# An attention output projection with Strassen's seven products for half of its rows of weights

## What is computed

```python
def mla(h, cos, sin, w_dq, q_norm_g, w_uq, w_dkv, kv_norm_g, w_ukv, w_o):
    ...
        outs.append(jnp.einsum('bhqk,bkhd->bqhd', p, v[:, :kend]))
    o = jnp.concatenate(outs, axis=1).reshape(B, S, H * V_HEAD_DIM)
    return o @ w_o

for i in range(DEPTH):                      # DEPTH = 2
    y = rmsnorm(h, attn_norm_g[i])
    y = conv_module(y, ...) if i == 0 else mla(y, ...)
    h = h + y
    h = h + swiglu(rmsnorm(h, ffn_norm_g[i]), ffn_w_gate[i], ffn_w_up[i], ffn_w_down[i])
return rmsnorm(h, final_norm_g)
```

## Time and profile before

| | us |
|---|---|
| median of 3 runs | 1991.01 |
| lowest, highest | 1988.06, 1994.06 |
| the profiled execution | 1993.24 |
| its span, first to last instruction | 1991.40 |

### The profile page before, as it was taken

One profiled execution on the slowest core, in us unless ns is written; L12 is line 12 of the kernel. 1 busy time (PEld: TensorE's weight loads), 2 busy tenths in 40 slices (PEclk: granted clock), 3 DMA queues, 4 the chain that ended last, 5 costly groups with the idle time before them and its releaser, 6 DMA issues.

```text
span 1991.4 us, 25065 instructions
## 1 busy us (share of the span) xinstructions
PE 1955.9 (98%) x9934; PEld 1671.0 (84%) x9934; DVE 1614.3 (81%) x1769; ACT 1141.2 (57%) x1138; POOL 227.7 (11%) x196
## 2 busy tenths in 40 slices
PE   8999899999999999999999999999999999999998
PEld 7999888888888888888888998888888888888886
DVE  6999886888888888888876775588888888888885
ACT  5898744555556555555544654355555555555553
POOL 0555400010011000110010000000010000101002
PEclk9999999999999999999999999999999999999999
DMA  8999464899998999889845444559989999999983
GB/s 272 257 259 236 148 214 148 240 271 278 254 235 241 261 279 262 223 242 263 258 145 151 123 143 174 190 174 287 243 216 273 259 279 239 236 253 262 277 211 127
DMA packets 253830, 453.37 MB, mean 228 GB/s; under 512 B 18708, under 2 KB 60444, under 8 KB 251420
## 3 DMA queue, kind: packets, MB, share of 16 engines
q1 hardware_dynamic: 207968, 349.73, 50.5%
q0 software_dynamic: 44256, 98.57, 28.8%
q10 hardware_dynamic: 1500, 3.61, 0.5%
HBM read 435.10 MB, written 2.10 MB: 220 GB/s over the span
## 4 chain that ended last, share of the span: by engine, by line
PE 87%; DMA 7%; DVE 3%; ACT 1%; issue 1%; SPq 0%; POOL 0%; ACTq 0%; DVEq 0%; POOLq 0%
PE ps L1802 83%; DMA raw<-in_conv_w_pw_dram 4%; DMA w_lo<-raw 3%; DVE ps L1311 1%; PE ps L2043 1%; ACT w_lo L772 1%; PE ps L2297 0%; PE ps L2298 0%; PE ps L2278 0%; DMA resid<-in_x_dram 0%; DVE w_lo L1188 0%; PE ps L1833 0%; SPq L557 0%; PE ps L1852 0%; PE ps L1841 0%
## 5 line engine op out<-in xcount | busy, mean ns | idle before, releaser
L1193 DVE TENSOR_TENSOR w_lo<-raw,w_hi 128x2048 fp32r<-128x2048 f32 x224 | 509.2, 2290 | 148.3 <-ACT w_hi L927 148.0
L927 ACT ACTIVATE w_hi<-raw 128x2048 fp32r<-128x2048 f32 x224 | 426.3, 1916 | 347.7 <-PE ps L1802 209.1
L1802 PE MATMUL ps<-w_hi,x_hi 128*128 128x512 f32 x1168 | 456.0, 390 | 0.9 <-DVE x_lo L1220 0.9
L1802 PE MATMUL ps<-w_hi,x_lo 128*128 128x512 f32 x1168 | 454.9, 389 | 0.0
L1802 PE MATMUL ps<-w_lo,x_hi 128*128 128x512 f32 x1168 | 454.8, 389 | 0.0
L1802 PE MATMUL ps<-w_hi,a_hi 128*128 128x512 f32 (+1 forms) x768 | 292.7, 381 | 0.0
L1802 PE MATMUL ps<-w_hi,a_lo 128*128 128x512 f32 (+1 forms) x768 | 292.3, 381 | 0.0
L1802 PE MATMUL ps<-w_lo,a_hi 128*128 128x512 f32 (+1 forms) x768 | 292.2, 380 | 0.0
L1802 PEld LDWEIGHTS ps<-w_hi,x_hi 128*128 128x128 f32 x1168 | 219.3, 188 | 47.1 <-DVE x_lo L1220 1.4
L1802 PEld LDWEIGHTS ps<-w_hi,x_lo 128*128 128x128 f32 x1168 | 219.3, 188 | 45.7
L1802 PEld LDWEIGHTS ps<-w_lo,x_hi 128*128 128x128 f32 x1168 | 219.3, 188 | 45.2
(11 more groups left out here) (242 smaller groups left out, 2992.7 us busy)
## 6 DMA issues: line engine op xcount, KB each, us to landing
raw<-in_ffn_w_down_dram SPq DMA_DIRECT2D x66, 1024.0 KB, 8.3
raw<-in_ffn_w_up_dram POOLq DMA_DIRECT2D x60, 1024.0 KB, 8.8
raw<-in_ffn_w_gate_dram SPq DMA_DIRECT2D x50, 1024.0 KB, 6.6
raw<-in_ffn_w_up_dram SPq DMA_DIRECT2D x48, 1024.0 KB, 6.4
row_bc<-in_ffn_w_gate_dram SPq DMA_DIRECT2D x38, 1024.0 KB, 5.9
raw<-in_conv_w_pw_dram SPq DMA_DIRECT2D x64, 512.0 KB
row_bc<-in_ffn_w_down_dram SPq DMA_DIRECT2D x22, 1024.0 KB, 5.8
b<-in_ffn_w_up_dram SPq DMA_DIRECT2D x40, 512.0 KB, 5.8
```

Source lines behind the costliest of these rows:

```text
L927: act.activation(f_w_tile(w_hi, l, q), f_raw_tile(l, q), ACT.Copy).then_inc(f_hi_done, 1)
L1193: dve.tensor_tensor(f_w_tile(w_lo, l, q), f_raw_tile(l, q), hi32(f_w_tile(w_hi, l, q)), ALU.subtract).then_inc(f_lo_done, 1)
L1802: ins = pe.matmul(dst, lhsT, rhs, start=first and n == 0, stop=last and n == len(pairs) - 1, skip_group_check=skip)
```

## The change

Rows 1024 to 2047 of `w_o` stay plain: 4 groups of 24 products for columns 0 to 1023 first (`group`), 4 places of 24 for the other columns (`P2`, `P3`, `M2`, `M3`, function `both`). Rows 0 to 1023 are done by seven products for each half of the columns: `A1` to `A7` and `B1` to `B7`, 14 places of one token tile, 12 products each (`place`). The left sides are blocks of `x` or the four sums `s_hi`, `s_lo`, which VectorE now makes here too (`x_sums` becomes `sums_of_x`). The right sides are blocks of `w_o` or sums of them: a block lies in `raw` or in `row_bc` (slot 4), is split and used, and then an adding transfer adds another block to it; eight places (`O_SUMS`) come from such a transfer, ten from a plain load (`o_load`). So 22 blocks are moved where 16 were. ScalarE copies six results out of PSUM to `scratch` (`o_copy`), VectorE makes 20 additions and subtractions. `pair_out` of the last pair moves ahead, behind the first group. The transposes for the feed-forward wait for three column blocks at once.

```diff
-G_END = {0: G_PW2 + CC * KG, 1: G_WO + CC * KG}
+G_END = {0: G_PW2 + CC * KG, 1: G_WO + KG}
+A1, A2, P2, A5, A3, B1, P3, A6, B5, A7, B3, A4, B6, M2, M3, B7, B2, B4 = range(18)
+O_SRC = {A1: (0, 0), A2: (0, 1), A5: (1, 0), A6: (1, 1), A4: (0, 1), A3: (1, 1), A7: (1, 0),
+         B1: (3, 0), B2: (3, 1), B5: (2, 0), B6: (2, 1), B4: (3, 1), B3: (2, 1), B7: (2, 0),
+         P2: (2, 2), P3: (2, 3), M2: (3, 2), M3: (3, 3)}
+O_RAW = {A1: 4, A5: 4, A6: 4, A4: 4, A3: 0, A7: 0, M3: 0, A2: 1, B3: 1, B7: 1, P2: 2, P3: 2, M2: 2, B2: 2,
+         B1: 3, B5: 3, B6: 3, B4: 3}
+O_SUMS = (A5, A6, A7, B5, A4, B6, B7, B4)
+O_ALL = 18
...
+def w_slot(l, slot):
+    return (slot + G_END[l] + O_ALL * l) % RING
...
+            def output_loads():
+                def o_load(p):
+                    before = o_before(p)
+                    if before is not None:
+                        sp.wait_ge(o_lo_done, before + 1)
+                    elif O_RAW[p] < RING:
+                        wait_lo(sp, G_WO + O_RAW[p])
+                    sp.dma_start(o_raw_tile(p).rearrange("p (k n) -> p k n", k=GK), o_src(p)).then_inc(o_in[O_RAW[p]], 16)
+                o_load(A1)
+                for n in range(KG):
+                    rows = slice(GK * (2 + n // 2), GK * (3 + n // 2))
+                    load(tile_rows(mla_w_o[0], rows, slice(CH * (n % 2), CH * (n % 2) + CH)), G_WO + n)
+                for p in (A3, A2, P2, B1, B3, P3, M2, M3, B2):
+                    o_load(p)
...
                     elif q < RING:
-                        wait_lo(sp, G_END[l] - RING + q)
+                        sp.wait_ge(o_lo_done, O_ALL - RING + q + 1)
...
+            for p in O_SUMS:
+                pool.wait_ge(o_lo_done, o_before(p) + 1)
+                pool.dma_start(o_raw_tile(p).rearrange("p (k n) -> p k n", k=GK), o_src(p),
+                               accum_op=ALU.add).then_inc(o_added[O_RAW[p]], 16)
...
+            def output_projection():
+                def o_hi(*places):
+                    for p in places:
+                        act.wait_ge(o_added[O_RAW[p]] if p in O_SUMS else o_in[O_RAW[p]], 16 * o_landed(p))
+                        if p < RING:
+                            act.wait_ge(group_used, G_WO + p + 1)
+                        else:
+                            act.wait_ge(o_used, p - RING + 1)
+                        act.activation(o_w_tile(w_hi, p), o_raw_tile(p), ACT.Copy).then_inc(o_hi_done, 1)
+                def o_copy(dst, bank, p):
+                    act.wait_ge(o_used, p + 1)
+                    act.activation(dst, ps[:, bank, :], ACT.Copy).then_inc(o_copied, 1)
+                o_hi(A1, A2)
+                act.wait_ge(o_sum_done, 1)
+                act.activation(s_hi[:, :, :, :].rearrange("p n k s -> p (n k s)"), ytmp[:, 1, :],
+                               ACT.Copy).then_inc(o_s_hi_done, 1)
+                o_hi(P2, A5)
+                o_copy(qa1, 4, A1)
+                o_hi(A3, B1, P3)
+                o_copy(qa5, 5, A5)
+                o_hi(A6, B5)
+                o_copy(qb1, 0, B1)
+                o_hi(A7, B3)
+                o_copy(qa16, 4, A6)
+                o_hi(A4)
+                o_copy(qb5, 3, B5)
+                o_hi(B6, M2, M3, B7)
+                o_copy(qb16, 0, B6)
+                o_hi(B2, B4)
+                for q in range(3):
+                    f_hi(1, q)
...
-            def square(g0):
-                for j in range(3):
-                    lo(g0 + 4 + j)
-                for n in range(CC):
-                    add_block(g0, n)
-                    if n < CC - 1:
-                        for g in range(g0 + KG * n + 7, min(g0 + KG * n + 11, g0 + KG * CC)):
-                            lo(g)
-                    if n == CC - 2:
-                        for q in range(3):
-                            f_lo(1, q)
+            def output_projection():
+                def o_lo(*places):
+                    for p in places:
+                        dve.wait_ge(o_hi_done, p + 1)
+                        dve.tensor_tensor(o_w_tile(w_lo, p), o_raw_tile(p), hi32(o_w_tile(w_hi, p)),
+                                          ALU.subtract).then_inc(o_lo_done, 1)
+                def add(n, t, part):
+                    cols = slice(CH * n, CH * n + CH)
+                    return dve.tensor_tensor(resid[:, t, cols], resid[:, t, cols], part, ALU.add)
+                sums_of_x(norm_counts(4) + KT, o_sum_done)
+                o_lo(A1, A2)
+                dve.wait_ge(o_s_hi_done, 1)
+                dve.tensor_tensor(s_lo[:, :, :, :].rearrange("p n k s -> p (n k s)"), ytmp[:, 1, :],
+                                  hi32(s_hi[:, :, :, :]).rearrange("p n k s -> p (n k s)"), ALU.subtract).then_inc(o_s_done, 1)
+                o_lo(P2, A5)
+                dve.wait_ge(group_used, G_WO + KG)
+                add(1, 1, ps[:, 3, :])
+                o_lo(A3)
+                dve.wait_ge(o_used, A2 + 1)
+                add(0, 0, ps[:, 0, :]).then_inc(o_mixed, 1)
+                dve.wait_ge(o_mixed, 1)
+                dve.wait_ge(o_copied, 1)
+                add(0, 0, qa1)
+                o_lo(B1, P3)
+                dve.wait_ge(o_used, A3 + 1)
+                add(1, 0, ps[:, 2, :])
+                o_lo(A6, B5, A7)
+                dve.wait_ge(o_copied, 4)
+                link(dve.tensor_tensor(qa16, qa5, qa16, ALU.subtract))
+                add(1, 0, qa16)
+                o_lo(B3, A4)
+                dve.wait_ge(o_used, A7 + 1)
+                add(0, 1, ps[:, 4, :])
+                dve.tensor_tensor(qa5, qa5, ps[:, 4, :], ALU.subtract).then_inc(o_mixed, 1)
+                dve.wait_ge(o_mixed, 2)
+                add(1, 1, qa5)
+                o_lo(B6)
+                dve.wait_ge(o_used, A4 + 1)
+                add(0, 1, ps[:, 1, :]).then_inc(out_added, 2 * TT)
+                o_lo(M2, M3)
+                dve.wait_ge(o_used, B3 + 1)
+                add(2, 0, ps[:, 6, :])
+                add(2, 1, ps[:, 7, :])
+                o_lo(B7)
+                add(3, 0, qb1)
+                dve.wait_ge(o_copied, 6)
+                link(dve.tensor_tensor(qb16, qb5, qb16, ALU.subtract))
+                add(2, 0, qb16)
+                o_lo(B2)
+                dve.wait_ge(o_used, B7 + 1)
+                add(3, 1, ps[:, 0, :])
+                link(dve.tensor_tensor(qb5, qb5, ps[:, 0, :], ALU.subtract))
+                add(2, 1, qb5).then_inc(out_added, TT)
+                o_lo(B4)
+                dve.wait_ge(o_used, B2 + 1)
+                add(3, 0, ps[:, 4, :])
+                for q in range(3):
+                    f_lo(1, q)
+                dve.wait_ge(o_used, B4 + 1)
+                add(3, 1, ps[:, 5, :]).then_inc(out_added, TT)
...
-                pe.wait_ge(out_added, added + TT * (n + 1))
+                pe.wait_ge(out_added, added + TT * (max(n, 2) + 1 if norm == 5 else n + 1))
...
+                def group(n):
+                    wait_lo(pe, G_WO + n)
+                    wh, wl = w_rows(w_hi, (G_WO + n) % RING), w_rows(w_lo, (G_WO + n) % RING)
+                    for kk in range(GK):
+                        k = GK * (2 + n // 2) + kk
+                        if kk % 2 == 0:
+                            pe.wait_ge(xlo_done, norm_counts(4) + k + 2)
+                        for t in range(TT):
+                            ah, al = x_tile(2 + n // 2, t)(kk)
+                            ins = product(ps[:, 2 * (n % 2) + t, :], three(ah, al, wh[:, kk, :], wl[:, kk, :]),
+                                          n < 2 and kk == 0, False, skip=True)
+                    ins.then_inc(group_used, 1)
+                def place(p, bank, lhs, first=False):
+                    pe.wait_ge(o_lo_done, p + 1)
+                    slot = (G_WO + KG + p) % RING
+                    wh, wl = w_rows(w_hi, slot), w_rows(w_lo, slot)
+                    for kk in range(GK):
+                        ah, al = lhs(kk)
+                        ins = product(ps[:, bank, :], three(ah, al, wh[:, kk, :], wl[:, kk, :]), first and kk == 0, False,
+                                      skip=True)
+                    return ins
+                def both(p, bank, j, first=False):
+                    place(p, bank, x_tile(j, 0), first)
+                    place(p, bank + 1, x_tile(j, 1), first).then_inc(o_used, 1)
+                group(0)
+                pair_out(PAIRS - 1)
+                for n in range(1, KG):
+                    group(n)
+                place(A1, 4, x_tile(0, 0), True).then_inc(o_used, 1)
+                place(A2, 0, x_tile(1, 0)).then_inc(o_used, 1)
+                both(P2, 6, 2, True)
+                pe.wait_ge(o_s_done, 1)
+                place(A5, 5, s_tile(1), True).then_inc(o_used, 1)
+                place(A3, 2, s_tile(4)).then_inc(o_used, 1)
+                pe.wait_ge(o_mixed, 1)
+                place(B1, 0, x_tile(0, 0), True).then_inc(o_used, 1)
+                both(P3, 6, 3)
+                pe.wait_ge(o_copied, 1)
```

(20 more changed lines are left out.)

93 lines of the change are left out of this document (60 added, 33 removed).

## The result

The changed kernel takes 2003.12 us, the median of 6 runs (2002.66 to 2006.61); the kernel before, on the same chip, 1991.26 (1988.06 to 1994.06). The ratio is 1.0063, 95% interval 1.0050 to 1.0076: 11.9 us slower by the medians, where 3.6 were forecast and the range ended at 2001.5.

A forecast was written before the change was run, and what follows sets the result against it. TensorE was taken to bound the kernel. New waits of 1.5+0.7+1.6+1.7+3.5 = 9.0 us against 5.4 saved gave +3.6, a median of 1994.6 us, range 1987.5 to 2001.5.

The forecast's parts named there:

- Saved 5.44: Output projection on TensorE: 384 products become 360, 24 fewer at 0.2267 us each, 5.44 us saved if all else stays hidden.
- Room on VectorE, 9 us: Output projection: VectorE's added work, 66.4 us of the 75 available, fits with 9 us to spare.
- Step 1: TensorE waits 1.4 to 1.6 us at B5, whose adding transfer queues behind those for A6 and A7.
- 8.4 after issue and 5.1 after the one ahead: Landing rule in the transfer walk: an adding transfer lands 8.4 us after issue, and 5.1 after the one ahead.
- Step 2: Wait at B3: VectorE's queue behind B5 needs 5.8 us against TensorE's 5.4; 0.7 us with handovers.
- Step 3: Wait at B6, which reuses B5's slot: 12.9 us between low parts against TensorE's 10.9; 1.5 us, plus 0.1 at M2.
- Step 4: Wait of 1.7 us ahead of B4, from VectorE's program order behind B7, whatever the transfers do.
- Step 5: TensorE idles 4.0 us before the feed-forward while VectorE finishes its queue; 0.45 before, so net 3.5.
- The clock: Rival: granted clock falls after the idle before the feed-forward, 2.7 to 3.4 us lost, +6.3 to +7.0 in all; chance 0.24.
- The rival of turns: Rival: plain loads B3, P3, M2 take turns with adding transfers, 8 us at B5, 2.5 at B6; about +12, 2003; chance 0.14.
- the load of 1347.46: Plain load in the trace before, issued 1.9 us behind an adding transfer; read as first come, first served.

The follow-up runs named there:

- e7: The change with its eight adding transfers made plain (no weight sums) and e2's reordered VectorE end: 1987.39 us, 0.9979 to the kernel before.
- e5: The change with e2's VectorE order, B3's load held until A5's transfer landed and M2's until B5's, P3's load ahead of B3's: 1995.02 us, ratio 1.0015.
- e1: The change with only M2's plain load held until B5's adding transfer has landed: 2002.60 us, ratio 1.0053 to the kernel before.
- e2: The change with only VectorE's program reordered at the stage's end (B4's low part earlier, two feed-forward low parts later): 1998.74 us, ratio 1.0030.
- e3: The change with 32 products that nobody reads put on TensorE between A6 and B5: 2003.83 us, ratio 1.0064 to the kernel before.
- e8: e6 with no load held (places reordered, e2's VectorE end, P3's load still ahead of B3's): 1993.06 us, ratio 1.0005 to the kernel before.
- e6: e5 with the places reordered on all engines: A6 ahead of P3, A7 ahead of B5, M2 ahead of B6: 1993.40 us, ratio 1.0006.
- e9: e6 with ScalarE's split of the feed-forward's third weight group moved behind x_hi's first chunk: 1990.63 us, ratio 0.9995 to the kernel before.

## Why the prediction was wrong

The sign of the sum was right, the size was not: +3.6 forecast, +11.9 measured, beyond the range. One step had a wrong mechanism, the price of the adding transfers ahead of B5.

- **Saved 5.44**: right. 24 products are gone, and with no transfer late e7 shows 4.5 of it.
- **Room on VectorE, 9 us**: right (e7: no wait over 0.5 in the stage).
- **Step 1, B5, 1.4 to 1.6**: measured 7.83. This is the step that failed, by 6.3 us: it took an adding transfer's time for fixed, whatever the other queue carries. Its rule "8.4 after issue and 5.1 after the one ahead" is right where the engines carry adding transfers alone: A6's landed after 8.4, and 1236 to 1242 gives 0.20 MB per us, 5.1 for one. It is wrong with a plain load in the other queue. A5's landed after 10.8, with B3's load issued 1.9 behind it: 2.4 late at the head of the chain (e5, without that load beside it, gives back 1.3; the other 1.1 stays open). Between A7's landing (1232.18+11.6 = 1243.8) and B5's (1235.71+16.8 = 1252.5) are 8.7 us, not 5.1: 3.6 more. A7's itself came 5.8 behind A6's: 0.7. Together 6.7. e1 and e5 show the two loads one by one: 4.5 and 1.2 us of B5's wait, 5.7 of the 6.3.
- **Step 2, B3, 0.7**: no wait; VectorE had the longer one at B5 to catch up in.
- **Step 3, B6, 1.5**: measured 1.32, but by luck: B6's transfer landed after 9.4, not 8.4, and step 2's 0.7 was missing, both of which lengthen the wait, while the half clock behind B5 kept TensorE 1.5 longer on the way.
- **Step 4, B4, 1.7**: 1.66. **Step 5, 4.0 before the feed-forward**: 3.74. Both right, and e2 shows that they are only VectorE's order.
- **The clock**, set to nothing with 0.24 on the rival: it fell at the end, 1.4 us, less than the 2.7 to 3.4 of that rival, and behind B5's wait, 1.5 by the accounting, of which e3 got back 0.2.
- **The rival of turns** (0.14) gave 2003 and was right in mechanism. That its number fits is in part luck. It had 2.7 us for each of three loads; M2's cost 4.3 of B5's landing (e1), B3's 1.3 of A5's (e5), P3's nothing that shows. Its 2.5 more at B6 did not appear, and the clock's 2.9, which it left out, did.

By terms: 3.6 + 6.3 at B5 - 0.7 at B3 - 0.3 at B6 - 0.2 at the end + 2.9 for the clock = 11.6, beside 12.4 for the stage and 11.9 for the medians.

The wrong reading was of the load of 1347.46. That it moved nearly nothing for some 4 us after its issue is true, and of M2's load too; that it did so until the adding transfer was through is not. I took the late start for an order of service. What decided was in the same row, 251 to 271 GB/s for 2 us ahead of the plain load's 389, and I named it and let it weigh too little. The queues of the trace before from 1352 to 1354, and the landing of the adding transfer of 1345.52:

```profile
q0 software_dynamic: 131, 0.26, 71.1%
q1 hardware_dynamic: 124, 0.25, 37.9%
...
DMA to landing us min/median/max: 11.2/11.2/11.2
```

Both moved, packet for packet, at the rate of 1242 to 1250 in the trace after (2.05 MB in 8 us, 256 GB/s), in which the adding transfer gets 0.135 MB per us instead of 0.20. And the longest landing of that trace, 11.2, which the prediction took as its upper bound, is this transfer's, with the load issued 1.9 us behind it: 2.8 over the best, as A5's was 2.4 over it. The price of one load was in the trace before.

## What to carry to other kernels

A transfer that adds should be priced by the bytes it moves per us beside what the other queues carry at that time, not by its landing in a quiet stretch, and what gives it room is distance in products between its issue and its use. Against e2, holding the loads (e5) brought the stage 3.6 us and the new order (e8) 5.2; but the new order moves M2's load away from B5's transfer as well, so for the distance by itself compare e6 with e5. Where a kernel's gain is 5 us, every engine's in-order program at the seam to the next stage needs its own walk; two orders there, VectorE's and ScalarE's, cost 5.3 to 6.5 and 2.4 us. Shortening a wait in the middle of a chain-bound stretch, by a held load (e1) or by filling TensorE (e3), brought a part of it back at the next place that hangs on the chain.

## What the runs showed that I had not expected

- An adding transfer of 1 MB occupies all engines for 5.1 us (0.20 MB per us), the same transfer without adding lands in 5.4 at best, and e7's two moved 1.68 MB in 5.5 us, gaps included. Its packets are half as large: 611 for 1.22 MB against 442 for 1.68.
- A plain load that meets adding transfers starts over 4 us after its issue and then takes its turns: M2's in the change, issued at 1237.64, had moved nothing by 1242, B3's, issued at 1216.00 with one adding transfer under way, 0.01 MB by 1220.4. B1's, issued at 1203.59 with none, was moving before 1205 and had landed after 5.0 us. Why the others start late was not tried.
- What a fall of the clock costs at the seam to the feed-forward: 3.4 us at half cost 1.4 (e6 against e9), 6.8 us cost 2.4 (e1's 47.24 for 192 products against e2's 44.87). The length of the idle time alone does not tell whether it falls: it fell at B6 after 2.23 us in e3 and not at B5 after 2.20 in e5, nor after 3.36 in e1. Behind a wait that a chain sets, a fall is nearly free (e3: 0.2 us of 1.5).
The Trainium skill, "TensorE: Matmul & The Clock Gate", Part 1, has the rule that an idle array drops to half rate and needs work to come back; the falls in the waits of 7.83 and 3.74 us agree.
